# Two loops of an SSD layer, the z projection and the scan with its output product, laid into one loop of eight like turns

## The reference

```python
proj = x @ w_in
z, xbc, dt = jnp.split(proj, [SSD_D_INNER, SSD_D_INNER + SSD_CONV_DIM], -1)
xbc = jax.nn.silu(causal_depthwise_conv(xbc, conv_w, conv_b))
xs, bm, cm = jnp.split(xbc, [SSD_D_INNER, SSD_D_INNER + SSD_N_GROUPS * SSD_D_STATE], -1)
dt = jax.nn.softplus(dt.astype(jnp.float32) + dt_bias).reshape(b, L, g, r)
a = -jnp.exp(a_log.astype(jnp.float32)).reshape(g, r)
...
decay = jnp.exp(segsum(adt))
cb = jnp.einsum('bclgn,bcsgn->bgcls', cc, bc)
y_diag = jnp.einsum('bgcls,bgrcls,bcsgrp->bclgrp', cb, decay, xdt)
...
y = y + d_skip.reshape(g, r)[..., None] * xs
yg = (y * jax.nn.silu(z.astype(jnp.float32))).reshape(b, L, g, SSD_NORM_GROUP)
yg = yg * lax.rsqrt(jnp.mean(yg * yg, -1, keepdims=True) + RMS_EPS)
yg = yg.reshape(b, L, SSD_D_INNER) * norm_g
return yg.astype(x.dtype) @ w_out
```

## Time and profile before

| | us |
|---|---|
| median of 3 runs (lowest, highest) | 2309.83 (2307.15, 2312.85) |
| profiled execution, its own time | 2313.82 |
| its span, first to last instruction | 2312.1 |
| TensorE busy in the span | 2116.1 (92%) |
| VectorE busy | 1363.8 (59%) |
| ScalarE busy | 1107.0 (48%) |
| mean granted TensorE clock | 0.964 |

### The profile page before, as it was taken

The page is one execution under the profiler, slowest core; times in us unless marked ns, Lnnn a source line. Parts: engine busy times, 40 slices in busy tenths (PEclk is TensorE's granted clock), DMA queues, the critical chain, the costliest instruction groups (busy, mean ns, idle before and its releaser), DMA issues.

```text
span 2312.1 us, 32966 instructions
## 1 busy us (share of the span) xinstructions
PE 2116.1 (92%) x13142; PEld 1891.5 (82%) x13142; DVE 1363.8 (59%) x1798; ACT 1107.0 (48%) x1493; POOL 37.9 (2%) x60
## 2 busy tenths in 40 slices
PE   4979999999999998999999978989798998888996
PEld 3768888879999787999988867778598998776885
DVE  4864764456655556666654436777756445665454
ACT  5842445544433344434344447766454345554333
POOL 0000000000000000000000000000000000000000
PEclk8889999999999999999999989999899999999998
DMA  9942543347775563555546553445363554233562
GB/s 343 332 154 91 182 146 114 105 146 273 274 249 184 185 198 122 187 177 177 183 135 199 187 176 111 161 159 185 98 200 115 183 183 144 74 107 116 195 197 76
DMA packets 204233, 394.61 MB, mean 171 GB/s; under 512 B 6726, under 2 KB 25916, under 8 KB 201692
## 3 DMA queue, kind: packets, MB, share of 16 engines
q1 hardware_dynamic: 199584, 369.78, 48.0%
q0 software_dynamic: 2880, 17.40, 2.1%
q10 hardware_dynamic: 1660, 5.90, 0.6%
HBM read 390.89 MB, written 2.16 MB: 170 GB/s over the span
## 4 chain that ended last, share of the span: by engine, by line
PE 71%; ACT 10%; DVE 10%; issue 6%; DMA 2%; ACTq 1%; DVEq 0%; POOL 0%; POOLq 0%
PE ps L1681 12%; PE ps L1683 11%; PE ps L1682 11%; PE ps L1669 10%; PE ps L1670 10%; PE ps L1671 10%; ACT w_hi L416 4%; DVE w_lo L933 2%; ACT actf L747 2%; DMA tables<-in_tables 1%; ACT actf L868 1%; PE ps L1841 1%; DVE sm L1508 1%; DVE actf L1505 1%; PE ps L1956 1%
## 5 line engine op out<-in xcount | busy, mean ns | idle before, releaser
L933 DVE TENSOR_TENSOR w_lo<-raw,w_hi 128x1024 fp32r<-128x1024 f32 (+1 forms) x676 | 813.5, 1219 | 729.2 <-ACT w_hi L416 728.6
L416 ACT ACTIVATE w_hi<-raw 128x1024 fp32r<-128x1024 f32 (+1 forms) x676 | 699.0, 1051 | 744.5 <-PE ps L1683 373.5
L1681 PE MATMUL ps<-act,w_hi 128*128 128x256 f32 x2048 | 588.2, 287 | 5.1 <-DVE w_lo L933 3.8
L1683 PE MATMUL ps<-act,w_lo 128*128 128x256 f32 x2048 | 581.5, 284 | 0.0
L1682 PE MATMUL ps<-act,w_hi 128*128 128x256 f32 x2048 | 581.4, 284 | 0.0
L1681 PEld LDWEIGHTS ps<-act,w_hi 128*128 128x128 f32 x2048 | 395.2, 193 | 9.0 <-DVE w_lo L933 4.6
L1682 PEld LDWEIGHTS ps<-act,w_hi 128*128 128x128 f32 x2048 | 395.1, 193 | 2.3 <-issue 2.2
L1683 PEld LDWEIGHTS ps<-act,w_lo 128*128 128x128 f32 x2048 | 395.0, 193 | 0.0
L1669 PE MATMUL ps<-w_hi,act 128*128 128x512 f32 (+1 forms) x896 | 353.5, 395 | 23.7 <-DVE act L1375 12.7
L1671 PE MATMUL ps<-w_hi,act 128*128 128x512 f32 (+1 forms) x896 | 348.8, 389 | 0.0
L1670 PE MATMUL ps<-w_lo,act 128*128 128x512 f32 (+1 forms) x896 | 348.8, 389 | 0.0
(11 more groups left out here) (282 smaller groups left out, 2412.4 us busy)
## 6 DMA issues: line engine op xcount, KB each, us to landing
raw<-in_ssd_w_in SPq DMA_DIRECT2D x80, 1024.0 KB, 5.1
raw<-in_w_in SPq DMA_DIRECT2D x72, 1024.0 KB, 5.2
raw<-in_w_ada SPq DMA_DIRECT2D x48, 1024.0 KB, 5.9
raw<-in_dsa_w_in SPq DMA_DIRECT2D x36, 1024.0 KB, 5.0
raw<-in_ssd_w_out SPq DMA_DIRECT2D x32, 1024.0 KB, 5.0
raw<-in_dsa_w_out SPq DMA_DIRECT2D x32, 1024.0 KB, 5.1
raw<-in_w_out SPq DMA_DIRECT2D x16, 1024.0 KB, 5.1
raw<-in_w_proj_a SPq DMA_DIRECT2D x12, 1024.0 KB, 5.1
```

Source lines behind the costliest of these rows:

```text
L416: e.activation(w_hi[:, nth(u) % SPLIT, :, :w], raw[:, t % RAW, 2 * h:2 * h + 2, :w], ACT.Copy).then_inc(hi_done, 1)
L933: e.tensor_tensor(w_lo[:, slot, :, :w], raw[:, t % RAW, 2 * h:2 * h + 2, :w], w_hi[:, slot, :, :w].bitcast(F32), ALU.subtract).then_inc(lo ...
L1681: e.matmul(o, wh, hi, start=first and f % 2 == 0, stop=False, skip_group_check=True)
L1683: ins = e.matmul(o, wl, hi, start=False, stop=last and f % 2 == 1, skip_group_check=True)
```

## The change

The z product and the output product now stand in one loop. z's first block stays by itself (`ssd_z`, 1 block); then 7 turns (`ssd_zo`) take 8 tiles each: block g of z, and the output product of group g-1; four tiles of the last group's output product follow. The decays, the running sums and silu(z) of one group lie in `gated` (`EX`, `RB`, `ZS`), the operands of the output product too, and x times dt overwrites x in its place, so `act` stays whole for z. Banks of PSUM: output 0 to 3, `cb` in bank 0, z in 4 and 5, y in 6 and 7.

On TensorE a turn is: units 0 and 1 of z, `cb` of g, z units 2 and 3, transposes of y of g-1, z units 4 to 7, the product y of g, and the 4 tiles of the output product of g-1. On ScalarE and VectorE one or two operations stand between splits; the 16 differences of the next group are spread over the turn in portions of 1 to 3, the last three in the next turn.

The product for `dt` moves into the x stage, ahead of its second block; its ScalarE and VectorE steps stand in the x and BC stages behind a convolution or between splits; ALPHA times x is taken in BC block 2; the differences and decays of group 0 are made in BC block 3. GpSimd's staging starts once `dt_ready` is there.

The diff, cut to the loops:

```diff
-    blocks("ssd_z", 8, 4)
-    blocks("ssd_out", 32, 1)
+    blocks("ssd_z", 1, 4)
+    blocks("ssd_zo", 7, 8)
+    blocks("ssd_out", 4, 1)
...
+            def scan_loads(i):
+                n0 = FIRST["ssd_zo"]
+                for j in range(4):
+                    load(n0 + j, i, i, 8)
                 for t in range(4):
...
+                for m in range(lo, lo + n):
+                    h, tt = m // 2, m % 2
+                    o = h * 384 + tt * 256
+                    w = 256 - tt * 128
+                    ins = e.activation(ex[:, o:o + w], rb[:, h * 256 + tt * 128:h * 256 + 256], ACT.Relu,
+                                       scale=-1.0, bias=sm[:, 76 + tt * 8 + h:77 + tt * 8 + h])
+                    if m % 8 == 7:
+                        ins.then_inc(S["diff_ready"], 1)
...
+            dt_exp()
+            for b in range(4):
+                ahead = 2 * FIRST["ssd_bc"] + 8 * b + 4
+                if b == 0:
+                    splits(ahead, 4)
+                    x_tokens(7, 1)
+                    splits(ahead + 4, 4)
+                if b == 1:
+                    splits(ahead, 6)
+                    dt_ln()
+                    splits(ahead + 6, 2)
+                if b == 2:
+                    splits(ahead, 2)
+                    e.activation(x[:, :, :], x[:, :, :], ACT.Copy, scale=ALPHA).then_inc(S["x_scaled"], 1)
+                    splits(ahead + 2, 6)
+                if b == 3:
+                    splits(ahead, 4)
+                    for m in range(4):
+                        splits(ahead + 4 + m, 1)
+                        differences(0, 4 * m, 4)
+                    decay(0, 0)
+                    decay(0, 1)
+                conv_silu(side[:, b * 1024:(b + 1) * 1024], 8, b)
+
+            splits(Z0 + 4, 8)
+            z_silu(ready("ssd_z", 0))
...
+                if not first:
+                    ahead(4)
+                    differences(g, 13, 3)
+                    ahead(5)
+                decay(g, 0)
+                if not first:
+                    ahead(6)
+                decay(g, 1)
+                if not first:
+                    ahead(7)
+                ahead(8)
+                y_high(g - 1)
+                ahead(9, 3)
+                z_silu(nth(ZO) + 8 + 16 * i)
+                ahead(12)
+                next_differences(0, 2)
+                ahead(13)
+                y_squares(g)
+                ahead(14)
+                next_differences(2, 3)
+                ahead(15)
+                y_root(g)
+                next_differences(5, 1)
+                ahead(16)
+                if last:
+                    y_scale(g)
+                    ahead(17)
+                    y_high(7, 4)
+                    ahead(18, 2)
+                else:
+                    next_differences(6, 3)
+                    ahead(17)
+                    y_scale(g)
+                    ahead(18)
+                    next_differences(9, 2)
+                    ahead(19)
+                    next_differences(11, 2)
+            scan_turn(1, 0)
+            with e.Fori(1, 6) as i:
+                scan_turn(i + 1, i)
+            scan_turn(7, 6)
...
+            for b in range(4):
+                splits(2 * FIRST["ssd_bc"] + 8 * b + 4, 8)
+                if b == 2:
+                    e.wait_ge(S["dt_turned"], 1)
+                    e.tensor_copy(t1[:, :], ps[:, 7, 0:256]).then_inc(S["dt_ready"], 1)
+                conv_bc(b, b % 2)
+                if b == 0:
+                    dt_parts()
+                if b == 1:
+                    dt_sums()
...
+                if not first:
+                    ahead(4, 3)
+                masked(g, 0)
+                if not first:
+                    ahead(7)
+                masked(g, 1)
+                weighted(g)
+                ahead(8)
+                y_low(g - 1)
+                ahead(9, 4)
+                y_gated(g)
+                ahead(13)
+                add(0)
+                ahead(14)
+                y_mean(g)
+                ahead(15)
+                add(1)
+                y_rstd(g)
+                ahead(16, 2)
+                if last:
+                    y_low(7, 4, 0)
+                add(2)
+                ahead(18, 2)
                 add(3)
-            each(e, G, scan_turn)
...
+            def x_block_dt(b, k, i, u0, step):
+                if k and isinstance(i, int):
+                    e.wait_ge(S["rows_loaded"], 16 * 5)
+                    dt_product()
+                x_block(b, k, i, u0, step)
...
+            gemm(Z0, 6, act, 4, True, ends=False)
+            e.wait_ge(dve_freed, OUT_FREED)
+            group_products(0)
+            gemm(Z0 + 6, 2, act, 4, True, kc0=12, starts=False)
+            y_product(0)
+
+            def scan_turn(g, i):
+                last = isinstance(i, int) and i == 6
+                e.wait_ge(act_freed, z_freed(g - 1))
+                gemm(ZO, 2, act, 4, True, i, 16, ends=False)
+                e.wait_ge(dve_freed, out_freed(4 * g - 6))
+                group_products(g)
+                gemm(ZO + 2, 2, act, 4, True, i, 16, kc0=4, starts=False, ends=False)
+                y_turn(g - 1)
+                gemm(ZO + 4, 4, act, 4, True, i, 16, kc0=8, starts=False)
+                y_product(g)
+                for t in range(4):
+                    if last and t == 3:
+                        y_turn(7)
+                    out_tile(t, g - 1, ZO + 8, i, 16)
+            each(e, 6, lambda i: scan_turn(i + 1, i))
+            scan_turn(7, 6)
```

More of the change, by code:

```diff
@@ L188, in build @@
     for seg, _, _, _, _ in TILES:
-        if seg not in ("head_q", "head_kv") and all(seg != s for s, _ in BLOCKS):
+        if seg == "ssd_zo" and all(seg != s for s, _ in BLOCKS):
+            for _ in range(7):
+                BLOCKS.append((seg, "act"))
+                BLOCKS.extend([(seg, "dve")] * 4)
+        elif seg not in ("head_q", "head_kv") and all(seg != s for s, _ in BLOCKS):
             nb = 1 + max(t[1] for t in TILES if t[0] == seg)
@@ L729, in _, with z_silu @@
[L729 to L739 removed]
+            Z0 = 2 * FIRST["ssd_z"]
+            ZO = 2 * FIRST["ssd_zo"]
+            U0 = 2 * FIRST["ssd_out"]
+            ex = gatedf[:, EX:EX + 3072]
+            rb = gatedf[:, RB:RB + 2048]
+            def z_silu(used):
+                e.wait_ge(units_used, used)
+                for n in range(2):
+                    e.activation(gatedf[:, ZS + n * 512:ZS + (n + 1) * 512], ps[:, 4 + n, :],
+                                 ACT.Silu).then_inc(act_freed if n == 1 else S["half_read"], 1)
@@ new lines, in _, with ahead, next_differences @@
+            splits(Z0 + 4, 8)
+            z_silu(ready("ssd_z", 0))
+            splits(ZO + 4, 1)
+            y_squares(0)
+            splits(ZO + 5, 1)
+            y_root(0)
+            differences(1, 0, 4)
+            splits(ZO + 6, 1)
+            y_scale(0)
+            differences(1, 4, 4)
+            splits(ZO + 7, 1)
+            differences(1, 8, 8)
+            def scan_turn(g, i):
+                def ahead(m, n=1):
+                    splits(ZO + m, n, i, 16)
+                first, last = isinstance(i, int) and i == 0, isinstance(i, int) and i == 6
+                def next_differences(lo, n):
+                    if not last:
+                        differences(g + 1, lo, n)
+                if not first:
[35 more added lines that the diff above has]
+                    next_differences(11, 2)
@@ new lines, in _, with scan_turn, ahead, add @@
+            splits(ZO + 5, 1)
+            y_mean(0)
+            e.wait_ge(S["x_scaled"], 1)
+            splits(ZO + 6, 1)
+            y_rstd(0)
+            splits(ZO + 7, 1)
+            def scan_turn(g, i):
+                def ahead(m, n=1):
+                    splits(ZO + m, n, i, 16)
+                def add(t):
+                    e.wait_ge(units_used, nth(ZO) + 10 + 2 * t + 16 * i)
+                    e.wait_ge(dve_freed, out_freed(4 * g - 8 + t))
+                    v = x[:, :, t * 512:(t + 1) * 512]
+                    e.tensor_tensor(v, ps[:, 2 * (t % 2):2 * (t % 2) + 2, :], v, ALU.add).then_inc(dve_freed, 1)
+                first, last = isinstance(i, int) and i == 0, isinstance(i, int) and i == 6
+                if not first:
[21 more added lines that the diff above has]
+                ahead(18, 2)
+                add(3)
@@ L2025, in scan_turn @@
-            def scan_turn(g):
-                later = not isinstance(g, int)
+            def x_block_dt(b, k, i, u0, step):
+                if k and isinstance(i, int):
+                    e.wait_ge(S["rows_loaded"], 16 * 5)
+                    dt_product()
+                x_block(b, k, i, u0, step)
+            segment("ssd_x", 4, 8, x_block_dt)
+            for b in range(4):
+                u0 = 2 * FIRST["ssd_bc"] + 8 * b
+                if b == 3:
+                    e.wait_ge(S["xt_copied"], 8)
+                    turn_dt()
+                pair_free(BI["ssd_bc"] + b)
```

(4 more changed lines are left out.)

364 lines of the change are left out of this document (152 added, 212 removed).

## The result

The changed kernel takes 2279.09 us (median of 4 runs, 2271.41 to 2281.76) against 2310.52 for the kernel before (median of 4, 2307.15 to 2312.85; the table of the kernel before has three of them). The ratio is 0.9859, with an interval of 0.9841 to 0.9877 (95%). That is 31.4 us less, where 27 were forecast (2283). The profiled execution took 2278.9, its span 2277.3.

A forecast was written before the change was run, and what follows sets the result against it. TensorE bounds z, a chain over all engines bounds the scan. 50 us idle or at half clock, less 13.5 (entry), 5 (clock) and 4 (BC), give 27: 2283 against the median 2309.8; range for 8 in 10: 2267 to 2301.

The forecast's parts named there:

- The turn: Steady loop: TensorE's work sets 50.8 us a turn, no waits in turns 2 to 7 or ahead of the last four tiles.
- The entry: Loop entry: three TensorE waits, 2.3 at z unit 4, 6.2 at group 0's transposes, 5.0 at the second product y; 13.5.
- The clock: Loop entry: TensorE's clock drops behind the waits, about 2 each for 6.2 and 5.0, 1 for the rest; 5 us.
- The BC stage and x: BC blocks 0 to 3 pay 0.9, 1.4, 0.9, 1.1 for moved work, sum 4; dt product moves to x at same price.
- the 50 to win: From the end of BC to the last output product, 50 us are idle or at half clock.
- The table loads: ScalarE: no extra drain after a load, going by the trace; by the skill's rule some 5 us more, sum 22.
- rivals 1 and 2: Rival 1: one old wait survives, 3.0 a turn, 2304 (0.12). Rival 2: both survive with clock drops, 2325 (0.07).
- Rival 3: Loop entry hidden too: its waits come to 5 and the clock stays up, 40 us less, 2270; chance 0.11.

The follow-up runs named there:

- the run that lost 2.7 there: Changed kernel with the first weighting operation of each turn on VectorE done four times (three repeats): 2331.81 us, 1.0095 to the kernel before.
- two repeats: Changed kernel with the first weighting operation of each turn on VectorE done three times: 2303.54 us, 0.9974 to the kernel before.

## Why the prediction was right

**The turn.** Right. Counted from `cb` to `cb` it is 50.53 against 50.8, five times, with no listed wait and a clock of 1.00; the last turn, with four more tiles, has no wait either. The loop has seven turns and not the title's eight, and the first of them holds the waits of the entry. Eight groups at 0.27 each make 2 us that the forecast didn't have. The old waits of the earlier trace rows are absent: the lead on the low operand is 1.1 (forecast 1.5), and the transposes moved back show that the place is what pays. The late add shows that the lead before tile 2 is a real limit too: the add moved 2.6 back (it stands at 1371.39 in the changed kernel, the next low part ends at 1374.0) and 1.6 to 1.7 came through, so the lead is about 1 (forecast 0.6).

**The entry.** The three places were right, the sizes too large: 0.97, 5.13 and 2.27, together 8.4, against 2.3, 6.2 and 5.0, together 13.5. The third was mis-sized most.

**The clock.** Sum term 5; measured 14.8 us at 0.50, which cost 7.4. The price of 1.6 a drop, from the 3.2 us of the earlier trace rows, was wrong for a wait ahead of the product y: there the drops in the like turns lasted 10 to 17 us and cost 4.9 to 7.2. In the forecast's own sum the two errors partly cancel: entry and clock 18.5, measured 15.8. The prediction read one slice below full clock in the middle of the earlier trace rows; there are two, the 24th and the 29th, and the second lies behind the layer and doesn't enter the sum.

**The BC stage and x.** Forecast 4, with something in each of four blocks: waits of 1.19, 1.39, 0.65 and none in block 3, which is 2.5 more than the three of 0.25 that were there before. Not foreseen was 1.60 in the x stage: the transposes of x wait there for ScalarE's read of the dt product, which stands behind a split that itself waits for TensorE, and which this block's banks don't need. With it z starts 5.2 later, counted from the transposes of x; the waits explain 4.1 of that, and the rest was not traced. One of the prediction's own signs of being wrong did show here: the x stage was to grow by no more than the 14.0 of the moved product. From the transposes of x to the last ones of the x stage it takes 224.9 instead of 209.0, 15.9 more. So the term of 4 came near the total with part of its cause wrong.

**Sum.** 50 and 2, less 8.4, 7.4 and 5.2, is 31.0; measured 31.2. The mechanism was right and the forecast of 27 is near for that reason, but its nearness is also in part luck: the entry's waits were 5.1 too large, the clock 2.4 and the stages ahead 1.2 too small, and the 50 to win were 2 short.

**The table loads.** In the turn the load at 1340.55 took 1.28 and the Exp behind it started at 1341.85, 0.02 later:

```profile
1340.55 1.28 ACT L768 ACT_TABLE_LOAD   x1
1341.85 1.49 ACT L768 ACTIVATE gatedf<-gatedf 128x1536 f32<-128x1536 f32 x1
```

By the drain that the Trainium skill adds to each switch ("ScalarE: Activation LUTs", section "What ACT_TABLE_LOAD costs") the next instruction would have come 1.4 later; this trace doesn't show it. Three loads a turn on ScalarE stayed hidden.

**The rivals.** None came. But rivals 1 and 2 were priced too low where the wait stands ahead of the product y. Had 3.0 a turn been lost there, the clock would have gone as well: the run that lost 2.7 there took 2332, not 2304. So had that lead failed by 3 us, the change would have made the kernel slower and not left it as it was. For a wait ahead of tile 2, waits of 1.6 to 1.7 a turn cost 11.4 and no clock. The forecast let the change turn slower from 5 us of lateness on VectorE's row; measured it lies between 2.5 (two repeats, 0.9974) and 3.8 (three, 1.0095). Rival 3 (the entry hidden as well) is what the new order gives: 2261.

## What to carry to other kernels

When two loops are laid into one, write the turn out and look for the smallest lead of an operand over the engine that needs it. Here that lead is 1.1 us; what is late beyond it costs itself and, ahead of the product y, another 5 to 7 us of clock in the turns where it fell. How finely the differences were portioned didn't matter. The first turn, in which nothing has a lead yet, needs an order of its own, which gave another 14 us on top of the change's 31 in two traces and 9 in a third, where the clock fell.

## What the runs showed of the hardware

- The clock can fall to 1.2 GHz after a wait of 1.4 us in an otherwise busy TensorE, and with equal waits it did so in every second turn. At the loop's entry it fell once behind a wait of 0.62 and twice stayed up behind the same wait.
- Behind waits up to 2.7 the fall begins while TensorE is busy again: 2.4 to 2.7 us after the end of the waits of 0.62 and 1.4, 0.7 to 2.3 after the end of those of 2.7. It lasts far longer than the wait: 10 us after 0.62 and after 1.4, 10 to 14 after 2.7.
- Waits of 1.6 to 1.7 ahead of tile 2 never made it fall (five turns at 1.00), nor did waits of 0.44 ahead of the product y in five turns. Why the place matters, and why the clock falls in some of like turns and not in others, stays open; one trace a kernel can't tell how often it does.
- The start of an unchanged part in the middle of the program lay anywhere within 8 us from kernel to kernel, while the like turns repeated to 0.1. The first turn repeated to 1.7 only (65.5 and 67.2), and in the new order it took 51.4 or 56.2.
- Repeats of a 128x1024 fp32 multiplication on VectorE, each waiting for the one before, ran at 1.26 us each, where one takes 1.22.
